# Two fused transformer blocks on one core: the latent attention's gate product spread over its turns

## The reference

```python
u = rms_norm(h, ln_w[l])                       # 16 meta rows + 512 rows
(cx, cb, cc, cz, cq, ckv, krope, mz, rq, rk, rv, rz) = jnp.split(u @ w_in[l], IN_OFFSETS, axis=-1)
y_conv = short_conv_mixer(cx, cb, cc, cz, conv_w[l], conv_b[l])
y_mla = mla_mixer(cq, ckv, krope, mz, ...)     # 8 heads, softmax, ends with o * jax.nn.silu(z)
y_ret = retention_mixer(rq, rk, rv, rz, ...)   # 4 heads, decay instead of softmax, o * silu(z)
y = jnp.concatenate([y_conv, y_mla, y_ret], axis=-1)
h = h + y @ w_out[l]
```

## Time and profile before

| | |
|---|---|
| median of 3 runs | 1410.03 us (1408.1 to 1413.98) |
| profiled execution | 1413.25 us, its span 1411.4 us |
| mean granted TensorE clock | 0.973 |
| TensorE busy | 1307.8 us, 93% of the span |
| VectorE, ScalarE, GpSimd busy | 648.0, 633.7, 408.6 us |
| DMA | 179.13 MB, mean 127 GB/s |

### The profile page before, as it was taken

One profiled execution on the slowest core, in us unless ns is written; L12 is line 12 of the kernel. 1 busy time (PEld: TensorE's weight loads), 2 busy tenths in 40 slices (PEclk: granted clock), 3 DMA queues, 4 the chain that ended last, 5 costly groups with the idle time before them and its releaser, 6 DMA issues.

```text
span 1411.4 us, 16952 instructions
## 1 busy us (share of the span) xinstructions
PE 1307.8 (93%) x6321; PEld 1005.8 (71%) x6321; DVE 648.0 (46%) x1424; ACT 633.7 (45%) x1104; POOL 408.6 (29%) x202
## 2 busy tenths in 40 slices
PE   5999989879899999999998998999999999899996
PEld 4788666557668766775787776888787777676764
DVE  4265354534320125334799435123533223678785
ACT  4443434343543446353532454432444323477771
POOL 4265221014554322222442222433304441100002
PEclk9999999979999999999999999999999999999998
DMA  4233423023445221221232121333106450799945
GB/s 154 72 112 92 159 83 131 18 66 115 142 120 173 76 60 46 75 60 46 76 111 75 54 60 53 98 134 104 53 1 213 164 189 12 308 391 412 419 158 196
DMA packets 76317, 179.13 MB, mean 127 GB/s; under 512 B 11184, under 2 KB 22758, under 8 KB 69574
## 3 DMA queue, kind: packets, MB, share of 16 engines
q1 hardware_dynamic: 68528, 164.96, 34.5%
q0 software_dynamic: 2592, 8.40, 1.6%
q10 hardware_dynamic: 5110, 4.62, 1.1%
HBM read 152.79 MB, written 25.17 MB: 126 GB/s over the span
## 4 chain that ended last, share of the span: by engine, by line
PE 43%; DVE 8%; ACT 2%; issue 1%; POOL 0%; DVEq 0%; ACTq 0%
PE ps L1027 10%; PE ps L1029 10%; PE ps L1028 10%; PE ps L1565 4%; DVE work L2725 1%; PE ps L1433 1%; PE ps L1416 1%; DVE dq L2734 1%; DVE best L2723 1%; PE ps L1389 1%; PE ps L1549 1%; DVE mix_lo L2504 1%; PE ps L1461 1%; PE ps L1423 1%; PE ps L1558 1%
## 5 line engine op out<-in xcount | busy, mean ns | idle before, releaser
L909 POOL TENSOR_TENSOR w_lo<-raw,w_hi 128x1024 fp32r<-128x1024 f32 (+1 forms) x158 | 378.5, 2412 | 779.9 <-ACT w_hi L1792 779.9
L1027 PE MATMUL ps<-w_hi,act_hi 128*128 128x512 f32 (+1 forms) x560 | 236.0, 421 | 7.2 <-POOL w_lo L909 3.9
L1792 ACT ACTIVATE w_hi<-raw 128x1024 fp32r<-128x1024 f32 (+1 forms) x158 | 159.1, 1032 | 161.6 <-PE ps L1029 153.3
L1028 PE MATMUL ps<-w_lo,act_hi 128*128 128x512 f32 (+1 forms) x560 | 220.8, 394 | 0.0
L1029 PE MATMUL ps<-w_hi,act_lo 128*128 128x512 f32 (+1 forms) x560 | 220.1, 393 | 0.0
L1027 PE MATMUL ps<-w_hi,mix_hi 128*128 128x512 f32 x320 | 131.7, 411 | 9.9 <-DVE mix_lo L2504 6.4
L1027 PEld LDWEIGHTS ps<-w_hi,act_hi 128*128 128x128 f32 (+1 forms) x560 | 105.5, 188 | 48.2 <-issue 14.8
L1029 PE MATMUL ps<-w_hi,mix_lo 128*128 128x512 f32 x320 | 126.2, 394 | 0.0
L1028 PE MATMUL ps<-w_lo,mix_hi 128*128 128x512 f32 x320 | 126.1, 394 | 0.0
L1029 PEld LDWEIGHTS ps<-w_hi,act_lo 128*128 128x128 f32 (+1 forms) x560 | 105.2, 188 | 25.5
L1028 PEld LDWEIGHTS ps<-w_lo,act_hi 128*128 128x128 f32 (+1 forms) x560 | 105.7, 189 | 24.3 <-issue 1.8
(11 more groups left out here) (472 smaller groups left out, 2130.1 us busy)
## 6 DMA issues: line engine op xcount, KB each, us to landing
raw<-in_w_in SPq DMA_DIRECT2D x92, 512.0 KB, 3.6
gu<-in_w_gate SPq DMA_DIRECT2D x16, 1024.0 KB, 7.7
gu<-in_w_up SPq DMA_DIRECT2D x16, 1024.0 KB, 9.9
dn<-in_w_down SPq DMA_DIRECT2D x16, 1024.0 KB, 9.9
x_rows<-zeros SPq DMA_DIRECT2D x16, 512.0 KB, 5.1
raw<-in_w_out SPq DMA_DIRECT2D x16, 512.0 KB, 4.3
raw<-in_w_mem_kv SPq DMA_DIRECT2D x16, 512.0 KB, 3.8
xe<-x_rows SPq DMA_DIRECT2D x15, 512.0 KB, 10.4
```

The lines of the kernel that those rows point to most:

```text
L909: pool.tensor_tensor(lo[:, 0:a], raw[:, g % RAW_SLOTS, 0:a], hi[:, 0:a].bitcast(F32), ALU.subtract).then_inc(*POOL.done(("w_lo", g)))
L1027: pe.matmul(dst, l_hi, r_hi, start=start, stop=False, skip_group_check=skip)
L1028: pe.matmul(dst, l_hi, r_lo, start=False, stop=False, skip_group_check=skip)
L1792: nc.scalar.activation(split_slot(g)[0][:, 0:a], raw[:, g % RAW_SLOTS, 0:a], ACTF.Copy).then_inc(*ACT.done(("w_hi", g)))
```

## The change

The gate product's 16 parts become the first entries of `fill`; every entry is now a single part or step, and a slot takes two of them (one in the fourth turn of a pair, and one more place behind each second transposes). ScalarE empties the gate's banks by plain copies and applies Silu later in one instruction of 2048 columns (`mla_gate`), in the fourth turn, in front of that turn's value products. The retention's steps and the first four parts of w_out0 come behind in the same list; three parts are left when the turns are over and run after the last value products.

```diff
@@ mla_order
-    fill = item("ret_qk", "ret_vz")
-    fill = [fill[i:i + 2] for i in range(0, len(fill), 2)]
+    fill = [[x] for x in item("mla_z", "ret_qk", "ret_vz")]
     fill[-1] += [("ret_start",)]
...
-    fill += [tail[0:2], tail[2:4]]
+    fill += [[x] for x in tail[0:4]]
...
-    order = [("mla_transposes", 0), ("mla_transposes", 1)]
+    order = [("mla_transposes", 0)] + take(1) + [("mla_transposes", 1)] + take(1)
     for m in range(turns + 1):
...
-                order += [("mla_transposes", 2 * m // NT)] + take() + [("mla_transposes", 2 * m // NT + 1)]
+                order += [("mla_transposes", 2 * m // NT)] + take(2) + [("mla_transposes", 2 * m // NT + 1)] + take(1)
             order += [("mla_scores", 2 * m)]
-        order += take()
+        n = 0 if m == turns else 1 if m % NT == NT - 1 else 2
+        order += take(n)
...
+        if m == NT - 1:
+            order += [("mla_gate",)]
         if m:
             order += [("mla_values", m - 1)]
-    while fill:
-        order += take()
+    order += take(len(fill))
@@ make_order
-    order += [("mla_norm", t) for t in range(2, NT + 1)] + item("mla_z")
+    order += [("mla_norm", t) for t in range(2, NT + 1)]
@@ ScalarE, evict
                 elif name == "mla_z":
                     act.wait_ge(*PE.after("acc", name, b))
-                    tables(SILU)
-                    nc.scalar.activation(z_mla[:, b, :], ps[:, b, :], ACTF.Silu).then_inc(*ACT.done(("z_mla", b)))
-                    if b == NT - 1:
-                        tables(LN_EXP)
+                    nc.scalar.activation(z_mla[:, b, :], ps[:, b, :], ACTF.Copy).then_inc(*ACT.done(("z_raw", b)))
@@ ScalarE, new
+            def mla_gate():
+                act.wait_ge(*ACT.after("z_raw", NT - 1))
+                tables(SILU)
+                nc.scalar.activation(z_mla[:, :, :], z_mla[:, :, :], ACTF.Silu).then_inc(*ACT.done(*[("z_mla", p) for p in range(4)]))
+                tables(LN_EXP)
```

More of the change, by code:

```diff
@@ L212, in mla_order, with take @@
     tail = item("w_out0")
-    fill += [tail[0:2], tail[2:4]]
-    def take():
-        return fill.pop(0) if fill else []
-    order = [("mla_transposes", 0), ("mla_transposes", 1)]
+    fill += [[x] for x in tail[0:4]]
+    def take(n):
+        taken = [x for f in fill[:n] for x in f]
+        del fill[:n]
+        return taken
+    order = [("mla_transposes", 0)] + take(1) + [("mla_transposes", 1)] + take(1)
     for m in range(turns + 1):
@@ L756, in item_readers @@
             if name == "mla_z":
-                return [(ACT, ("z_mla", b))]
+                return [(ACT, ("z_raw", b))]
             if name == "ret_qk":
@@ L2365, in _ @@
             steps = {"mla_sums": mla_sums, "mla_scores": mla_scores, "mla_turn": mla_turn, "ret_start": ret_start,
-                     "ret_transposes": ret_transposes, "ret_values": ret_values, "ret_turn": ret_turn, "ret_norm": ret_norm, "mix_mla": mix_mla, "mix_ret": mix_ret, "gla_low": gla_low, "gla_decays": gla_decays,
+                     "ret_transposes": ret_transposes, "ret_values": ret_values, "ret_turn": ret_turn, "mla_gate": mla_gate, "ret_norm": ret_norm, "mix_mla": mix_mla, "mix_ret": mix_ret,
+                     "gla_low": gla_low, "gla_decays": gla_decays,
                      "gla_turn": gla_turn, "gla_values": gla_values, "mix": mix, "idx_key": idx_key,
```

## The result

The changed kernel takes 1423.35 us (median of 6 runs, 1421.66 to 1428.94), the kernel before 1413.90 over its six. The ratio is 1.0086, with a 95% interval of 1.0066 to 1.0105: slower by 0.86%, some 12 us (the two medians alone lie 9.5 us apart). The forecast was 1410.3 us and no change.

A forecast was written before the change was run, and what follows sets the result against it. The prediction took TensorE, busy 93% of the span, as the bound, so its idle or lower-clock time counts. Terms -11.9 + 1.8 + 4.1 - 4.2 + 1.9 + 8.6 = +0.3 us gave 1410.3 us, no change; range 1401 to 1419.

The forecast's parts named there:

- the gate product leaves its place: Before the first transposes: 22.3 us of parts go, TensorE waits 10.4 us for q's rotation; -11.9 us.
- start to first scores: First transposes to first scores: two transpose sets and two parts, partly at the lower clock, 6.9 us; +1.8 us.
- turns 0 to 3: Gate parts replace ret_qk parts; the gate's Silu makes TensorE wait 5.2 us, plus 1.7 lower clock; +4.1 us.
- turns 4 to 7: One part fewer, waits at scores(8) go, rotations of rq and rk fall on turns 6 and 7 for 1.8; -4.2 us.
- turns 8 to 11: Parts replace retention steps: 34.0 us of work, 4.6 idle, 1.0 for the rest of the rotations; +1.9 us.
- the rest up to the last value products: Last stretch: all of the retention, 39.8 us of work, two steps to a slot waiting 10.2; +8.6 us.
- behind them: After the last value products: three leftover parts where TensorE waited 2.83 us for mix_lo; nothing taken for them.
- 0.8 for bank 4: In the last stretch: one of the retention's waits, 0.8 us of the 10.2 in all.
- The slow one: Last stretch: the 3.0 us wait before the second values drags the clock down, 8 us more, 1418; chance 0.15.
- The waits are smaller than I add them: Gate and retention waits: no lower clock, part caught up, retention waits half as long; -8.7, about 1401.5; chance 0.25.
- The rotation stays at 2.5 us: At the start: slow rotation instructions hold TensorE until 140.3, +8.5 us, 1418.8; chance 0.05.
- One sign that I gave: End of the last value products: the prediction is wrong if they end more than 6 us from 306.

The follow-up runs named there:

- a_again: The changed kernel itself, no edit, in a second set of 6 runs: 1.0090 times the kernel before.
- a_no_rot: The changed kernel with VectorE's rotations of rq and rk replaced by one copy per tile: 1.0050 times the kernel before.
- a_apart_held: Changed kernel, parts dealt out by turn 10, retention one step a slot, each rq/rk rotation behind the next turn's copy on VectorE: 1.0019 times the kernel before.
- a_packed_held: a_apart_held with the retention's steps two to a slot again, up to turn 12: 1.0115 times the kernel before.
- a_all2: Changed kernel, q's rotation and convolution copies out of the start, Silu behind exp(8), retention one step a slot, rq/rk rotations behind next turns' copies: 1396.27 us, 0.9899.
- a_held: The changed kernel with, on VectorE alone, each of the four rotations of rq and rk behind the next turn's copy: 1.0102 times the kernel before.

## Why the prediction was wrong

The prediction's terms against a_again, both as differences to the kernel before, in us:

| term | forecast | measured |
|---|---|---|
| the gate product leaves its place | -11.9 | -11.4 |
| start to first scores, and turns 0 to 3 | +5.9 | +5.0 |
| turns 4 to 7 | -4.2 | +2.2 |
| turns 8 to 11 | +1.9 | +3.1 |
| the rest up to the last value products | +8.6 | +14.8 |
| behind them | 0 | -0.9 |
| sum (of unrounded terms) | +0.3 | +12.9 |

**"The gate product leaves its place": right.** The wait is 10.74 us where 10.4 was forecast, the rotations run at 0.42 us since GpSimd had nothing to subtract. The step missed that the convolution's copy would have held the second transposes 5 us later anyway; that changed nothing as long as the rotation came last, and is why removing the wait alone gave back half.

**"Start to first scores" and "Turns 0 to 3": right.** The start took 7.7 us where 6.9 were forecast (134.86 to the first scores at 142.59), turns 0 to 3 then 36.0 against 33.6, which is the +4.1 without the lower clock behind the gate. The gate's wait is 4.40 us instead of 5.2, with 1.0 at the lower clock behind it, where I had 1.7; it falls behind the cut, into turns 4 to 7. The Silu took 1.91 us (worked out: 1.98) and each load 1.28 with the next instruction right behind it, as in the earlier trace rows. The 1.38 us drain that the Trainium skill, ScalarE: Activation LUTs, What ACT_TABLE_LOAD costs, counts with each switch did not show: the instruction before the first load ended at 173.37, 0.03 us ahead of it. The measurement decides.

**"Turns 4 to 7": the step that failed.** I let the rotations fall on turns 6 and 7 (by the list they stand in turns 7 and 8: the last parts of ret_qk follow scores(14), scores(15) and the transposes of head 4), where "prob(14) is late, so exp(15), so copy(14), which I work out as 1.8". What was late was something smaller: VectorE's copy of turn 13's meta rows, which stands behind prob(14) and whose bank scores(15) claim. That is a wait of 4.97 us and twice the time for the matmuls behind it. I had read that claim in the retention ("0.8 for bank 4") and not in turn 7. The one rotation beside GpSimd, 2.57 us, is in it too: I had priced that contention at the start only, where there is none. a_no_rot puts the whole of the rotations at 5.9 us in these turns, 5.6 by the ratio, where I had 1.8. That is 4.1 of the 6.4 by which the term missed; another 1.0 is the gate's lower clock, which I had booked ahead of the cut, and 1.3 stay open.

**"The rest up to the last value products": the mechanism was right, its size was not.** The term missed by 6.2 us, nearly as much as turns 4 to 7. The waits came out as forecast in sum, 9.7 us in a_again against 10.2, but not singly: the first was 0.8 where I had 1.7, the one in front of the second values 2.3 instead of 3.0, those of the last turns 3.2 instead of 1.9. So the sum is better than its parts, and that is luck. What was mis-sized is the own work: 39.8 us forecast, 45.6 measured up to the end of the last values (every start-to-start distance less its wait). Retention 19.2 instead of 17.0, of which some 1.6 are value products at the lower clock after the 2.3 us wait; turns 17.4 instead of 14.4; parts 9.0 instead of 8.4. The turns' products are thus the largest error. It isn't the clock: in a_apart_held, at a clock of 1.00, the same turns take 17.9. I summed them from places where they followed each other and not where short ones start behind waits; that this is the reason is not shown. The 0.9 us gained behind the stretch are the last value products themselves, 1.02 us here and 1.87 before, where they ran at the lower clock.

**"Turns 8 to 11":** 1.2 us more, by two errors that nearly cancel. The waits are 3.4 us, where I had put 5.6 of idle time; the own work is 37.5 instead of 34.0 (turns 13.6 for 12.4, parts 23.8 for 21.6), the same kind of error as in the last stretch.

**The rivals.** The slow one named the place, but not the size: it wanted a clock drawn down to the end, 8 us of work at half. The value products behind the wait did run at half (16 in 3.94 us instead of some 2.4), but the stretch's clock was 0.94 to 0.97, not half. It was right that a wait of 2.3 us there is followed by the lower clock. "The waits are smaller than I add them" was wrong: the gate's wait and its lower clock were 1.5 us less and the retention's waits 0.5, where it wanted 8.7. "The rotation stays at 2.5 us" did not happen at the start, but it did once in turn 7. The range, 1401 to 1419, left out what happened: it was built from the terms that I had, and not from one that I had at 1.8 us and that was 5.9. One sign that I gave decides it: the last value products end 17 us behind 306, of which 2.5 were there before the change.

What stays open: how much of the last stretch's excess in the changed kernel is the packing itself. a_apart_held is 16.3 us shorter there, but 10.1 of it is work that now stands ahead of the cut (parts 7.2, the retention's first transposes and scores 2.9). The other 6.2 us are mostly waits, 5.0 instead of 9.7, and 1.9 of the retention's own products, which take 17.3 us in all at a clock of 1.00. Since the parts were dealt out otherwise too, this is an estimate of what packing costs; a_packed_held, 14.5 us, bounds it from above. Whether GpSimd's subtraction alone, moved away from the rotation, would have saved 2 of the 5 us in turn 7 was not tried.

## What to carry to other kernels

Dealing out a block of product that stands in front of a chain moves the chain's start ahead of everything that the block was hiding; look for every producer that ends inside the block, not only the last, since behind the first there is a second. And a step that is moved needs its deadlines looked up on both sides: what stands behind it on its engine, down to the smallest copy, and who needs the bank that it empties. Here the idea was worth 1%, but only once five neighbours had been moved with it (q's rotation, the convolution's copies, the gate's Silu, the retention's steps, the rotations of rq and rk); each remedy alone left the kernel slower than, or level with, the one before.

## What the runs showed of the hardware that I had not expected

- The large waits repeat, the clock doesn't. The gap at the start was 10.74 or 10.75 us in all ten executions that had it, the one in turn 7 4.95 to 4.97 in six. A piece at half clock in the last stretch was there in some and not in others, and is worth 1.7 us (54.3 or 56.0).
- TensorE came out of 10.7 us of idleness at half clock: four transposes took 1.09 us instead of 0.60, the part behind them had records of 0.63 us instead of 0.39. After the 5 us gaps it was the same, after one of 0.73 us it was not. After a wait of 3.0 us both were seen: the scores behind it took 2.13 us in a_all2 and 1.16 in a_apart_held.
- VectorE's instruction with two SBUF inputs took 2.57 us beside GpSimd's subtraction and 0.42 without, and 1.61 where they overlapped in part (a_held, at 231.05 us); on the 16 meta rows it was 2.40 beside it (a_all2) and 0.28 without (a_held, at 227.39 us). In each it ended 0.15 to 0.3 us behind GpSimd's instruction. The ones with one input in PSUM stayed at 0.40 to 0.42 us beside it: at 180.45 and 180.78 us in the kernel before (GpSimd from 179.84 for 2.36), at 230.29 and 230.62 in a_held (from 230.01 for 2.37). The Trainium skill, SBUF — State Buffer, SBUF: two separate sides, says that VectorE with two SBUF inputs and GpSimd reading SBUF exclude each other, that whichever starts first keeps the shared ports for its whole instruction, and that the other is blocked; the traces agree.
